# Expert loads on two queues, stores one block later, and a token operand kept in PSUM

## The chip, the cores and the metric

The kernel runs on one core of a Trainium2 chip. The metric is the device time of one execution in microseconds. Three runs of the kernel before gave 5060.06, 5060.66 and 5067.99 us (median 5060.66).

## The reference, cut to what matters

The layer first mixes tokens (attention, a Fourier branch, gates), then mixes channels with PEER, a retrieval over 128 x 128 = 16384 single-neuron experts. The change is in PEER alone:

```
q = hf @ wq                                  # 512 tokens, 8 heads, 2 halves
s = einsum(q, keys);  s1, s2 = top 16 of each half
idx, w = top 16 of the 16 x 16 sums, softmax # 8 x 16 = 128 experts per token
a    = einsum('td,thkd->thk', hf, u[idx])    # up: one dot of length 2048 per pair
coef = w * gelu(a)
out  = einsum('thk,thkd->td', coef, v[idx])  # down
```

All is fp32. `u` and `v` are 16384 x 2048, 134 MB each.

## The kernel before, in words

**Two ways through the experts.** The last 384 tokens (`TD`) are computed densely: for each of the 128 blocks of 128 experts the whole block of `u` is read and multiplied with all 384 tokens, Gelu is applied, and the result goes to a scratch in HBM (`gelu_d`); a second scratch (`route_d`) holds the routing weights, and the down phase multiplies the two. The first 128 tokens (`TS`) are computed sparsely: for each of the 128 slots (head, rank) one row of `u` per token is gathered by an indirect DMA and dotted with that token.

**One dense block i.** `pre_load` (L550) on SyncE issues four DMAs of 256 KB from `peer_u`, one for each quarter of the model dimension; quarter k goes to partitions 32k to 32k+31 of `pu[i % 2]`. VectorE transposes the block in two halves (`u_turn`, L1602, a STREAM_TRANSPOSE of 128 x 1024 into `pT`), ScalarE rounds each half to `pTuh` (`pre_hi`, L1066), GpSimd subtracts to get the low part `pTul` (`u_low`, L718), and TensorE does 48 matmuls of 384 columns (`pre_quarter`, L2232; three products for each of 16 chunks). ScalarE applies Gelu (`pre_gelu`, L1072), and SyncE stores 192 KB (`pre_store`, L557). Every buffer in this line exists twice.

**What sets the order.** Every engine has its order written out by hand, with semaphore waits. Three matter here:

- SyncE (L571 to L632): load of block i+2, store of block i, load of i+3, store of i+1, and so on. The load of i+2 waits until block i has been turned; the store of i waits for Gelu of i (`gelu_set`), and everything behind it on SyncE waits with it.
- ScalarE (`up_block`, L1084): `pre_hi` of block i+1, second half; `pre_hi` of block i+2, first half; then Gelu of block i.
- VectorE: the turn of block i+1's second half may start when the matmuls of block i-1 are done, that of i+2's first half when those of the first half of block i are done.

**Stages of the up phase.** Blocks 0 to 39: VectorE also finds the top experts, four groups of tokens one after the other in stretches of ten blocks (`top_experts`, L1617, with the turns put between its steps); TensorE waits for its end after blocks 19, 29 and 39. Blocks 40 to 63: VectorE also builds one-hot tiles (`one_hots`, L1695), TensorE multiplies them into routing tiles, ScalarE copies these (`keep_route`, L1105), SyncE stores them in pieces of 1 MB (`route_store`, L561); the last four follow after block 63. Blocks 64 to 127 (`LATE` = 64): from block 66 on GpSimd issues gathers of 128 rows of 8 KB (1 MB) into a ring of four buffers (`gather_u`, L727), three per block for four blocks, then two per block; VectorE does one dot for each (`dot`, L1723, a SCALAR_TENSOR_TENSOR of 128 x 2048 with a sum). The ring buffers lie over `route`, so the first gather waits for the last route store. At block 70 SyncE also loads the first operands of the down phase (two `vraw` of 1 MB, two `wt` and two `gel` of 384 KB).

**The token operand.** The matmul operand `h2h`/`h2l` has the model dimension on partitions; chunk c holds, on partition 32w + r, the dimension 512w + 32c + r. The dots need it by token. `tokens_turn` (L2250) turns it on TensorE in blocks 2 to 5: 32 matmuls of 128 columns into the first four PSUM banks, and ScalarE copies them (L1097, in blocks 6 to 9, with the order of the dimension put right) to `h2tok` in SBUF, as [128, 16, 512] of which the first 128 columns of each chunk are used.

Of the kernel before, what the change touches and what calls it, by code (L numbers as in the profile page):

```python
# [119 lines left out]
def layer_kernel(nc, a, out):  # L120
# [10 lines left out]
    with ctx:  # L131
# [119 lines left out]
        h2tok = sb("h2tok", 104, [P, DC, T])  # L251
# [34 lines left out]
        pp = [ctx.enter_context(nc.psum_tensor(f"pp{k}", [P, 1024], fp32)) for k in range(4)]  # L286
# [77 lines left out]

        wmod_v = a["w_mod"][0].rearrange("(c p) n -> p c n", p=P)
# [16 lines left out]
        def _(sp):  # L382
# [161 lines left out]
            u_v = a["peer_u"][0].rearrange("(i j) d -> i j d", j=NK)  # L544
            v_v = a["peer_v"][0].rearrange("(i j) d -> i j d", j=NK)
            u_quarter = [u_v[:, :, QD * k:QD * k + QD].rearrange("i (b s) d -> i s b d", s=32) for k in range(4)]
# [3 lines left out]
            def pre_load(i, s):  # L550
                if not isinstance(i, int) or i >= 2:
                    sp.wait_ge(u_turned, 2 * i - 2)
                for k in range(4):
                    sp.dma_start(pu[s][32 * k:32 * k + 32, :, :],  # L554
                                 u_quarter[k][bass.ds(i, 1)].rearrange("a s b d -> (a s) b d")).then_inc(u_in[s], 16)
# [15 lines left out]
            with sp.Fori(0, P0 // 2) as i:  # L571
                for s in range(2):
                    pre_load(2 * i + 2 + s, s)
                    pre_store(2 * i + s, s)
# [4 lines left out]
            def route_steps(r, first=False):  # L579

                for k in range(8):
                    i = 8 * r + P0 + k
                    pre_load(i + 2, k % 2)
                    if k >= 4:
                        route_store(32 * r + 16, 0, k - 4)
                    elif not first:
                        route_store(32 * r, 1, k)
                    pre_store(i, k % 2)
# [4 lines left out]
            pre_load(LATE + 2, 0)  # L593
            for k in range(4):
                route_store(GROUPS, 1, k)
            pre_store(LATE, 0)
            pre_load(LATE + 3, 1)
            pre_store(LATE + 1, 1)
            with sp.Fori(LATE // 2 + 1, LATE // 2 + 3) as i:
                for s in range(2):  # L600
                    pre_load(2 * i + 2 + s, s)
                    pre_store(2 * i + s, s)
# [26 lines left out]
            with sp.Fori(LATE // 2 + 3, NK // 2 - 1) as i:  # L629
                for s in range(2):  # L630
                    pre_load(2 * i + 2 + s, s)
                    pre_store(2 * i + s, s)  # L632
# [126 lines left out]
        def _(act):  # L759
# [305 lines left out]

            def pre_hi(i, s, h):  # L1066
# [9 lines left out]

            act.wait_ge(mu_red, 64)
            act.activation(identr[:, :], ident[:, :], ACT.Copy)
            pre_hi(0, 0, 0)
            pre_hi(0, 0, 1)  # L1080
            pre_hi(1, 1, 0)
# [28 lines left out]
            def route_part(r):  # L1110

                for k in range(8):
# [3 lines left out]
                    pre_hi(i + 1, 1 - s, 1)  # L1116
# [1267 lines left out]
```

## Time and profile before

| what | us |
|---|---|
| median of three runs | 5060.66 |
| the profiled execution, its own time | 5068.84 |
| its span, first to last instruction | 5067.2 |
| first Gelu of the up phase to the last | 2293.8 to 3860.6 |
| blocks 40 to 63 | about 2750 to 3060 |
| down phase to the end | about 3865 to 5067 |

All times inside the trace are counted from the start of the span. A row of the trace gives the start, the duration, the engine, the line of the kernel and the operation with its output and inputs. SPq, ACTq and so on are an engine's queue, where waits and DMA issues stand. "Releaser" is what ended a wait. A busy share of DMA is the mean over the 16 DMA engines; q1 is the queue of the DMAs that SyncE issues, q0 that of GpSimd's.

### The profile page before, as it was taken

To read this page: it belongs to the slowest core of one execution; us is meant where nothing else is said; L and a number is where in the kernel's file an instruction comes from. 1 tells how busy PE (TensorE), PEld (TensorE's weight loads), DVE (VectorE), ACT (ScalarE), POOL (GpSimd) and SP (SyncE) were. 2 spreads that over 40 slices of the span, in tenths; PEclk is the share of its full clock that TensorE was granted. 3 is DMA by queue.
4 is the path that set the end of the run, shared out by engine and by line. 5 is a ranking of instruction groups with operands and counts; after the bars stand their busy time and mean duration, and the time that the engine had idled before them with its cause. 6 is when DMAs were issued, how large, how long until landed. Compare 5 with 4: busy or idle time off the path is not lost.

```text
span 5067.2 us, 58390 instructions
## 1 busy us (share of the span) xinstructions
PE 4391.1 (87%) x21067; PEld 3686.3 (73%) x21067; DVE 3052.9 (60%) x3412; ACT 1381.0 (27%) x1489; POOL 1591.9 (31%) x643
## 2 busy tenths in 40 slices
PE   7899999999979976898777996677777799999997
PEld 2687777777768865778777996677776677777776
DVE  1234565455436535457667995566665677787777
ACT  0322332333321121322223442122222233332222
POOL 0002331000003300224444435677774233333330
PEclk9899999999999988899999998999999899999998
DMA  8325663000116552664444779899997889989895
GB/s 280 91 83 169 181 185 116 30 29 19 35 55 193 179 125 73 151 142 108 109 107 100 167 175 257 266 281 279 280 282 260 304 335 335 336 329 341 327 343 179
DMA packets 716548, 967.20 MB, mean 191 GB/s; under 512 B 137467, under 2 KB 535859, under 8 KB 680371
## 3 DMA queue, kind: packets, MB, share of 16 engines
q1 hardware_dynamic: 675395, 680.41, 46.3%
q0 software_dynamic: 40928, 285.23, 15.2%
q8 instruction: 45, 0.74, 0.1%
q10 hardware_dynamic: 144, 0.52, 0.0%
q14 instruction: 36, 0.29, 0.0%
HBM read 896.84 MB, written 69.22 MB: 191 GB/s over the span
## 4 chain that ended last, share of the span: by engine, by line
DMA 22%; DVE 13%; issue 7%; SPq 5%; PE 4%; ACT 1%; POOL 0%; DVEq 0%; ACTq 0%; POOLq 0%
DMA gel<-gelu_scratch 11%; DMA pu<-in_peer_u_dram 11%; DVE acc L1749 3%; DVE oneJ L1700 3%; DVE pT L1607 3%; SPq L554 3%; DVE vDl L1418 3%; PE pp L115 1%; PE pp L116 1%; PE pp L117 1%; ACT act_g L1075 1%; SPq L559 1%; SPq L608 0%; SPq L615 0%; DVE oneI L1701 0%
## 5 line engine op out<-in xcount | busy, mean ns | idle before, releaser
L115 PE MATMUL pp<-h2h,pTuh 128*128 128x384 f32 x2048 | 736.3, 360 | 270.3 <-POOL pTul L721 269.4
L721 POOL TENSOR_TENSOR pTul<-pT,pTuh 128x1024 fp32r<-128x1024 f32 x256 | 695.5, 2718 | 603.0 <-ACT pTuh L1070 601.6
L116 PE MATMUL pp<-h2l,pTuh 128*128 128x384 f32 x2048 | 711.0, 347 | 0.0
L117 PE MATMUL pp<-h2h,pTul 128*128 128x384 f32 x2048 | 711.0, 347 | 0.0
L115 PE MATMUL pp<-vDh,coh 128*128 128x512 f32 x1536 | 614.6, 400 | 97.6 <-DVE col L1418 97.2
L115 PEld LDWEIGHTS pp<-h2h,pTuh 128*128 128x128 f32 x2048 | 404.8, 198 | 312.8 <-POOL pTul L721 286.3
L116 PE MATMUL pp<-vDl,coh 128*128 128x512 f32 x1536 | 608.7, 396 | 0.0
L117 PE MATMUL pp<-vDh,col 128*128 128x512 f32 x1536 | 607.3, 395 | 0.0
L1607 DVE STREAM_TRANSPOSE pT<-pu 128x1024 f32<-128x1024 f32 x256 | 317.2, 1240 | 449.2 <-DMA pu<-in_peer_u_dram 385.7
L1070 ACT ACTIVATE pTuh<-pT 128x1024 fp32r<-128x1024 f32 x256 | 271.5, 1060 | 1146.7 <-DVE pT L1607 1146.4
L697 POOL TENSOR_TENSOR mbuf<-mbuf,silu 128x2048 f32<-128x2048 f32 x64 | 261.1, 4080 | 1003.6 <-DMA mbuf<-in_w_mod_dram 1002.9
L735 POOL DMA_INDIRECT ring<-in_peer_v_dram,sidx x128 | 337.2, 2634 | 752.5 <-DVE acc L1749 732.9
L1137 ACT ACTIVATE vDh<-vraw 128x2048 fp32r<-128x2048 f32 x128 | 245.3, 1917 | 670.9 <-PE pp L117 441.0
L1213 DVE TENSOR_TENSOR wl<-wraw,wh 128x2048 fp32r<-128x2048 f32 (+1 forms) x97 | 263.0, 2711 | 270.0 <-ACT wh L797 269.9
L115 PEld LDWEIGHTS pp<-vDh,coh 128*128 128x128 f32 x1536 | 294.9, 192 | 178.8 <-DVE vDl L1418 76.5
L116 PEld LDWEIGHTS pp<-h2l,pTuh 128*128 128x128 f32 x2048 | 405.7, 198 | 0.0
L117 PEld LDWEIGHTS pp<-h2h,pTul 128*128 128x128 f32 x2048 | 403.8, 197 | 0.0
L1725 DVE SCALAR_TENSOR_TENSOR ring<-ring,h2tok 128x2048 f32<-128x2048 f32 x128 | 359.2, 2810 | 0.0
L117 PEld LDWEIGHTS pp<-vDh,col 128*128 128x128 f32 x1536 | 294.9, 192 | 63.3
L116 PEld LDWEIGHTS pp<-vDl,coh 128*128 128x128 f32 x1536 | 295.3, 192 | 60.6
L1418 DVE TENSOR_TENSOR vDl<-vraw,vDh 128x2048 fp32r<-128x2048 f32 x128 | 292.7, 2287 | 64.7 <-ACT vDh L1137 64.6
L115 PE MATMUL pp<-hxh,wh 128*128 128x512 f32 x784 | 316.3, 404 | 13.7 <-DVE wl L1213 9.8
(329 smaller groups left out, 8152.4 us busy)
## 6 DMA issues: line engine op xcount, KB each, us to landing
pu<-in_peer_u_dram SPq DMA_DIRECT2D x512, 256.0 KB, 5.1
vraw<-in_peer_v_dram SPq DMA_DIRECT2D x128, 1024.0 KB, 9.5
mbuf<-in_w_mod_dram SPq DMA_DIRECT2D x64, 1024.0 KB, 5.9
wraw<-in_w_in_dram SPq DMA_DIRECT2D x48, 1024.0 KB, 8.6
wt<-route_scratch SPq DMA_DIRECT2D x128, 384.0 KB, 9.0
gel<-gelu_scratch SPq DMA_DIRECT2D x128, 384.0 KB, 10.4
wm<-in_w_mod_dram SPq DMA_DIRECT2D x16, 2048.0 KB, 8.8
gelu_scratch<-act_g SPq DMA_DIRECT2D x128, 192.0 KB, 1.9
```

What stands on the lines that cost most here:

```text
L115: pe.matmul(out, lh, rh, start=first, stop=False)
L116: pe.matmul(out, lh, rl, start=False, stop=False)
L117: return pe.matmul(out, ll, rh, start=False, stop=last)
L697: pool.tensor_tensor(mbuf[s][:, :, :], mbuf[s][:, :, :], silu[:, :, 0:1].to_broadcast([P, DC, P]), ALU.mult).then_inc(mu_prod, 1)
L721: pool.tensor_tensor(pTul[s][:, c, :], pT[s][:, c, :], pTuh[s][:, c, :].bitcast(fp32), ALU.subtract).then_inc(u_lo, 1)
L735: pool.indirect_dma_start(ring[k % 4][:, :], None, v_rows, bass.IndirectOffsetOnAxis(ap=sidx[:, k:k + 1], axis=0)).then_inc(ring_in[k % 4] ...
L1070: act.activation(pTuh[s][:, 8 * h:8 * h + 8, :], pT[s][:, 8 * h:8 * h + 8, :], ACT.Copy).then_inc(u_hi, 1)
L1137: act.activation(vDh[s][:, :, :], vraw[s][:, :, :], ACT.Copy).then_inc(w_hi, 1)
L1213: dve.tensor_tensor(wl[s][:, 0:n, :], wraw[s][:, 0:n, :], wh[s][:, 0:n, :].bitcast(fp32), ALU.subtract).then_inc(w_lo, 1)
L1418: return dve.tensor_tensor(dst, src, hi.bitcast(fp32), ALU.subtract)
L1607: dve.transpose(pT[s][:, c, :].rearrange("p c (b j) -> p b c j", b=4), pu[s][:, :, 256 * h:256 * h + 256].rearrange("p b (c j) -> p b c j" ...
L1725: dve.scalar_tensor_tensor(out=chunks(ring[k % 4]), in0=chunks(ring[k % 4]), scalar=1.0, in1=h2tok[:, :, 0:TS], op0=ALU.mult, op1=ALU.mult ...
```

## The change

**Loads.** `pre_load` on SyncE issues quarters 0 and 1 only. ScalarE gets a `pre_load` of its own for quarters 2 and 3 (its own DMA queue); it does blocks 0 and 1 before the up phase, block 2 after the first `pre_hi`s, and in `up_block` and `route_part` the load of block i+3 directly behind `pre_hi` of block i+1's second half.

**Stores.** SyncE starts with the loads of blocks 0 to 3 and the store of block 0; from there load i+2 is followed by the store of i-1 instead of i. The route stores are put in three groups instead of four, and the last four come behind the store of block 64 instead of behind the load of block 66.

**Token operand.** `h2tok` is now the first 2048 columns of PSUM (the four banks that `tokens_turn` writes). `tokens_turn` writes it in natural order: each of the 32 matmuls becomes four of 32 columns. The four copies on ScalarE are gone, and the dots read PSUM.

```
@@ layer_kernel
-        h2tok = sb("h2tok", 104, [P, DC, T])
-        pp = [ctx.enter_context(nc.psum_tensor(f"pp{k}", [P, 1024], fp32)) for k in range(4)]
+        ps = ctx.enter_context(nc.psum_tensor("ps", [P, 4096], fp32))
+        pp = [ps[:, 1024 * k:1024 * k + 1024] for k in range(4)]
+        h2tok = ps[:, 0:D]
@@ sync
             def pre_load(i, s):
                 if not isinstance(i, int) or i >= 2:
                     sp.wait_ge(u_turned, 2 * i - 2)
-                for k in range(4):
+                for k in range(2):
...
             pre_load(0, 0)
             pre_load(1, 1)
-            with sp.Fori(0, P0 // 2) as i:
+            pre_load(2, 0)
+            pre_load(3, 1)
+            pre_store(0, 0)
+            with sp.Fori(1, P0 // 2) as i:
                 for s in range(2):
                     pre_load(2 * i + 2 + s, s)
-                    pre_store(2 * i + s, s)
+                    pre_store(2 * i + s - 1, 1 - s)
...
                     pre_load(i + 2, k % 2)
-                    if k >= 4:
-                        route_store(32 * r + 16, 0, k - 4)
-                    elif not first:
-                        route_store(32 * r, 1, k)
-                    pre_store(i, k % 2)
+                    pre_store(i - 1, (k - 1) % 2)
+                    if k >= 5:
+                        for part in ((0, 1), (2,), (3,))[k - 5]:
+                            route_store(32 * r + 16, 0, part)
+                    elif 1 <= k < 4 and not first:
+                        for part in ((0, 1), (2,), (3,))[k - 1]:
+                            route_store(32 * r, 1, part)
...
             pre_load(LATE + 2, 0)
+            pre_store(LATE - 1, 1)
+            pre_load(LATE + 3, 1)
+            pre_store(LATE, 0)
             for k in range(4):
                 route_store(GROUPS, 1, k)
-            pre_store(LATE, 0)
-            pre_load(LATE + 3, 1)
-            pre_store(LATE + 1, 1)
@@ scalar
+            def pre_load(i, s):
+                for k in range(2, 4):
+                    act.dma_start(pu[s][32 * k:32 * k + 32, :, :],
+                                  u_quarter[k][bass.ds(i, 1)].rearrange("a s b d -> (a s) b d")).then_inc(u_in[s], 16)
...
-            def up_block(i, s, exp=None):
+            def up_block(i, s, exp=None, load=True):
                 pre_hi(i + 1, 1 - s, 1)
+                if load:
+                    pre_load(i + 3, 1 - s)
...
-                if 6 <= i < 10:
-                    k = i - 6
-                    act.wait_ge(h2_turned, DC + 4)
-                    act.activation(h2tok[:, :, 0:TS].rearrange("p (a k) (c r) -> p k a c r", a=4, c=4)[:, k],
-                                   pb[k][:, :].rearrange("p (c a r) -> p a c r", c=4, a=4), ACT.Copy).then_inc(h2_hi, 1)
@@ vector
-                dve.scalar_tensor_tensor(out=chunks(ring[k % 4]), in0=chunks(ring[k % 4]), scalar=1.0,
-                                         in1=h2tok[:, :, 0:TS], op0=ALU.mult, op1=ALU.mult,
+                dve.scalar_tensor_tensor(out=ring[k % 4][:, :], in0=ring[k % 4][:, :], scalar=1.0, in1=h2tok, op0=ALU.mult, op1=ALU.mult,
                                          accum_out=dots[:, k:k + 1]).then_inc(ring_used, 1)
@@ tensor
-                    o = pb[k][:, P * (c % 4):P * (c % 4) + P]
-                    pe.matmul(o, h2h[:, c, 0:TS], identr[:, :], start=True, stop=False)
-                    mm = pe.matmul(o, h2l[:, c, 0:TS], identr[:, :], start=False, stop=True)
+                    for w in range(4):
+                        o, e = pb[w][:, 32 * c:32 * c + 32], identr[:, 32 * w:32 * w + 32]
+                        pe.matmul(o, h2h[:, c, 0:TS], e, start=True, stop=False)
+                        mm = pe.matmul(o, h2l[:, c, 0:TS], e, start=False, stop=True)
```

## Rows read from the trace of the kernel before

**Rows 1.** Windows: stretch, length, busy of PE, PEld, DVE, ACT, POOL; clock, DMA share, GB/s.

```profile
2293.80:2745.00 451.20, 356.98 (x1910) 345.24 (x1908) 311.07 (x885) 111.53 (x133) 205.80 (x78) 0.93 0.46 108
2750.00:3060.40 310.40, 307.29 (x1932) 285.67 (x1931) 306.18 (x527) 149.38 (x167) 126.52 (x48) 1.00 0.73 164
3060.40:3208.50 148.10, 92.18 (x461) 89.31 (x460) 72.35 (x52) 23.24 (x29) 86.69 (x39) 0.82 0.91 271
3208.50:3846.10 637.60, 494.92 (x2545) 467.15 (x2544) 413.42 (x319) 132.31 (x160) 497.53 (x212) 0.95 0.94 278
```

**Rows 2.** Timeline of PE in block 3 (matmuls of one block, then of the turn).

```profile
2311.06 0.39 PE L115 MATMUL pp<-h2h,pTuh 128*128 128x384 f32 x1
...
2319.44 0.22 PE L2253 MATMUL pp<-identr,h2h 128*128 128x128 f32 x1
...
2319.61 0.27 PE L2253 MATMUL pp<-identr,h2h 128*128 128x128 f32 x1
2319.72 0.28 PE L2254 MATMUL pp<-identr,h2l 128*128 128x128 f32 x1
```

**Rows 3.** The chain of waits, 2533 to 2560: start, us, what.

```profile
2538.53 6.28 DMA pu<-in_peer_u_dram
2544.93 1.26 DVE pT L1607
...
2547.17 0.48 ACT act_g L1075
2547.81 0.37 SPq L559
...
2548.47 0.32 SPq L554
```

**Rows 4.** The chain of waits, 3400 to 3440.

```profile
3407.66 7.62 DMA pu<-in_peer_u_dram
...
3420.61 6.58 DMA pu<-in_peer_u_dram
```

**Rows 5.** The span.

```profile
core 0 of [0], span 5067.2 us
```

**Rows 6.** Waits in 2273 to 2765: total us, times, longest.

```profile
PE pp L2267 <- DVEq L1691: 42.5, 3, 14.6
```

**Rows 7.** Timeline of SP, then of POOL, at the boundary after block 63.

```profile
3063.59 14.12 SPq L566 DMA_DIRECT2D route_scratch<-route  x4
...
3084.34 1.09 POOL L730 DMA_INDIRECT ring<-in_peer_u_dram,sidx  x1 [19.12 <-DMA route_scratch<-route]
```

**Rows 8.** DMA queues in 4000 to 4800, the down phase.

```profile
q1 hardware_dynamic: 50830, 170.11, 59.2%
q0 software_dynamic: 13687, 99.62, 31.1%
```

**Rows 9.** DMA queues in 3208.5 to 3846.1: packets, MB, share of 16 engines.

```profile
q0 software_dynamic: 15277, 111.25, 50.5%
q1 hardware_dynamic: 38160, 66.01, 43.2%
```

**Rows 10.** DMA queue q1 in 2293.8 to 2745.

```profile
q1 hardware_dynamic: 28080, 48.57, 46.3%
```

**Rows 11.** DMA queue q1 in 900 to 1300, loads over all 128 partitions.

```profile
q1 hardware_dynamic: 6336, 11.01, 8.1%
```

**Rows 12.** Groups by shape: VectorE with one operand in PSUM.

```profile
L1382 DVE TENSOR_TENSOR pTl<-pp,pTh 128x768 fp32r<-128x768 f32 x64 | 61.0, 953 | 49.7 <-ACT pTh L894 48.9
L1334 DVE TENSOR_TENSOR kTl<-pp,kTh 128x512 fp32r<-128x512 f32 x24 | 16.6, 692 | 72.6 <-ACT kTh L868 72.6
```

**Rows 13.** Groups in 3200 to 3800: busy us, mean ns; idle before.

```profile
L721 POOL TENSOR_TENSOR pTul<-pT,pTuh 128x1024 fp32r<-128x1024 f32 x101 | 283.4, 2806 | 118.4 <-ACT pTuh L1070 117.4
...
L1725 DVE SCALAR_TENSOR_TENSOR ring<-ring,h2tok 128x2048 f32<-128x2048 f32 x100 | 276.5, 2765 | 0.0
L730 POOL DMA_INDIRECT ring<-in_peer_u_dram,sidx x100 | 189.3, 1893 | 15.6 <-issue 12.9
```

**Rows 14.** The gathers of u (L730), issue to landing.

```profile
DMA to landing us min/median/max: 5.4/7.9/13.1
```

More of the change, by code:

```diff
@@ L363, in layer_kernel @@
         block = ctx.enter_context(nc.Block())
+        u_v = a["peer_u"][0].rearrange("(i j) d -> i j d", j=NK)
+        u_quarter = [u_v[:, :, QD * k:QD * k + QD].rearrange("i (b s) d -> i s b d", s=32) for k in range(4)]
         wmod_v = a["w_mod"][0].rearrange("(c p) n -> p c n", p=P)
@@ L542, in _ @@
             sp.dma_start(iota[:, :], a["k_iota"]).then_inc(iota_in, 16)
-            u_v = a["peer_u"][0].rearrange("(i j) d -> i j d", j=NK)
             v_v = a["peer_v"][0].rearrange("(i j) d -> i j d", j=NK)
-            u_quarter = [u_v[:, :, QD * k:QD * k + QD].rearrange("i (b s) d -> i s b d", s=32) for k in range(4)]
             for ss in g_stored:
@@ L601, in _ @@
                     pre_load(2 * i + 2 + s, s)
-                    pre_store(2 * i + s, s)
+                    pre_store(2 * i + s - 1, 1 - s)
             def v_load(n, s, half):
@@ L631, in _ @@
                     pre_load(2 * i + 2 + s, s)
-                    pre_store(2 * i + s, s)
+                    pre_store(2 * i + s - 1, 1 - s)
+            pre_store(NK - 3, 1)
             pre_store(NK - 2, 0)
@@ L1075, in pre_gelu @@
                 act.activation(act_g[s][:, :], pb[4 + s][:, 0:TD], ACT.Gelu).then_inc(gelu_set, 1)
+            act.wait_ge(sc_done, 2 * PH)
+            pre_load(0, 0)
+            pre_load(1, 1)
             act.wait_ge(mu_red, 64)
@@ L1080, in _ @@
             pre_hi(0, 0, 1)
+            pre_load(2, 0)
             pre_hi(1, 1, 0)
-            def up_block(i, s, exp=None):
+            def up_block(i, s, exp=None, load=True):
                 pre_hi(i + 1, 1 - s, 1)
+                if load:
+                    pre_load(i + 3, 1 - s)
                 if exp is not None:
@@ L1116, in route_part @@
                     pre_hi(i + 1, 1 - s, 1)
+                    pre_load(i + 3, 1 - s)
                     for q in range(RI):
@@ L1125, in _ @@
                 route_part(r)
-            with act.Fori(LATE // 2, NK // 2 - 1) as i:
+            with act.Fori(LATE // 2, NK // 2 - 2) as i:
                 for s in range(2):
                     up_block(2 * i + s, s)
+            up_block(NK - 4, 0)
+            up_block(NK - 3, 1, load=False)
             pre_hi(NK - 1, 1, 1)
@@ L1717, in _ @@
                     route_block(2 * r + P0 + s, s, 8 * r + 4 * s)
-            def chunks(t):
-                return t[:, :].rearrange("p (c d) -> p c d", c=DC)
             def dot(k):
                 dve.wait_ge(ring_in[k % 4], 16 * (k // 4) + 16)
-                dve.scalar_tensor_tensor(out=chunks(ring[k % 4]), in0=chunks(ring[k % 4]), scalar=1.0,
-                                         in1=h2tok[:, :, 0:TS], op0=ALU.mult, op1=ALU.mult,
+                dve.scalar_tensor_tensor(out=ring[k % 4][:, :], in0=ring[k % 4][:, :], scalar=1.0, in1=h2tok, op0=ALU.mult, op1=ALU.mult,
                                          accum_out=dots[:, k:k + 1]).then_inc(ring_used, 1)
-            dve.wait_ge(h2_hi, DC + 4)
+            dve.wait_ge(h2_turned, DC + 4)
             for i in range(LATE, NK):
```

## The prediction

> **What bounds the kernel now.** Everything that the diff touches lies in the up phase, so I read that phase alone. The windows [rows 1] cut it in four; dividing the matmul counts by 48 per block (less 32 for the token turn in the first) gives 39, 24, 9 to 10 and 53 blocks. So a block takes 451.2/39 = 11.6 us beside the top-expert search, 310.4/24 = 12.9 us beside routing, and 637.6/53 = 12.0 us beside the gathers. Against that TensorE needs 8.38 us for a block at full clock: from 2311.06 to 2319.44 it runs one without a gap [rows 2]. In the first and last stretch it is thus idle or slow for a quarter to a third of the time, and VectorE is no bound either (311 of 451 us, 413 of 638).
>
> The chain of waits says what is. In the first stretch [rows 3] it is a closed loop through a single load: the Gelu (0.48 us) lets the store go (0.37), the load is issued behind it (first of four issues at 2548.47), its data take 6.28 us after the last issue, the turn 1.26, and the next Gelu can only come behind the rounding of that turn, because ScalarE's order puts it there. From Gelu to Gelu in such a loop it is 11 to 12 us. Beside the gathers the same loop stands with 7.62 and 6.58 us of transfer [rows 4]. In the routing stretch VectorE is busy 306 of 310 us [rows 1]: no load ends a wait there that matters. In the last stretch the DMA engines are busy 0.94 of the time [rows 1], so there the loop has a second bound close behind it.
>
> **The change part by part.** The profiled execution (5068.8 us, its span 5067.2 [rows 5]) stands 8.2 us above the median of 5060.66; I sum against the first and subtract 8 at the end.
>
> *Store one block behind the load, stretch 1.* Load i+3 now needs Gelu i-1 and the turn of i+1, which is where load i+2 stood before. It is thus issued one block earlier in relation to its use, and the closed loop spans two blocks: 11.6/2 = 5.8 us per block, no longer a bound. Next late are TensorE at 8.38 us and VectorE at 311/39 = 8.0 us. Two engines so evenly loaded, one of them with steps of uneven length between its turns, don't overlap perfectly. I take 39 x 8.38 = 327, 4 for two waits at ends of the search (now 14 us each [rows 6], because the last turn waits for the same loads; then about 2), 8 for uneven steps, and 8 for the token turn (below): 347 us, a gain of 104. Bounds: 39 x 8.38 + 4 = 331 (gain 120) and 10.0 us per block = 390 (gain 61).
>
> *Two loads on ScalarE.* Two issues of 0.32 us plus gaps, about 1 us per block on an engine busy 112 of 451 us here and 149 of 310 beside routing [rows 1]: hidden by its idle time; if that were gone it would cost 1 us per block. What queues behind them is the next rounding, and behind that GpSimd and TensorE, which then have a block's time in hand.
>
> *Token turn and its copies.* 128 matmuls for 32. The 128-column ones stand 0.11 us apart [rows 2], most of it the change of weights, which stays. Upper bound 96 x 0.11 = 10.6 us, lower 0 if they scale with columns; I take 8, nearer the row. The four copies leave ScalarE's idle time: nothing.
>
> *Routing stretch.* VectorE's work is the same: 0. The route stores move among the loads; half a block of lateness is hidden by a slot being free for four blocks.
>
> *Boundary, 3060 to 3208.* The first gather waits 19.12 us for the last route stores, which SyncE issues from 3063.59 during 14.12 us [rows 7] with two loads behind them. Now they follow the store of block 64, some 8 us later; the loads of 66 and 67 stand ahead of them. The stretch moves 148.1 x 271 GB/s = 40.1 MB. At 335 GB/s, about what the down phase moves ((170.1 + 99.6) MB / 800 us = 337 [rows 8]), that takes 120 us: 28 less, minus 8 = 20 us. Bounds 0 and 35.
>
> *Beside the gathers, 53 blocks.* The loop is gone here too, and the DMA engines become the bound, so their time per MB decides. Now: q1 0.432 x 637.6/66.0 = 4.17 us per MB, q0 0.505 x 637.6/111.3 = 2.89 [rows 9]; per block 1.245 and 2.10 MB, so 5.19 + 6.08 = 11.27 us of work in 12.03. In stretch 1, with nothing beside them, the same loads cost 4.30 us per MB [rows 10], while loads that spread one DMA over all 128 partitions cost 0.081 x 400/11.0 = 2.94 [rows 11]: what is slow is the form, each quarter into 32 partitions, one after another. With quarters 0, 1 on one queue and 2, 3 on the other, two sets of partitions are written at once. If that undoes the loss wholly (2.94, and 2.50 for gathers as in the down phase [rows 8]) the work is 3.66 + 5.25 = 8.9 us, 9.5 at today's share of 0.94; if not at all it is 11.27, 11.5 at a share of 0.98. I take the middle of the two works, 10.1, at 0.98: 10.3 us per block, a gain of 53 x 1.73 = 92. Bounds 28 and 134.
>
> Here row and skill part. The loads' rows above suggest that two halves written at once run faster. The Trainium skill, SBUF — State Buffer, section "Can I just issue two DMAs to hit both halves?", says that one DMA on each half of the partitions gained only 6% over a single one, from whichever engines they are issued. By that rule the DMA work stays, and the result is the first rival's. No row of this case has two such queues.
>
> *Dots from PSUM.* VectorE with one operand in PSUM takes 692 ns for 512 elements and 953 for 768 [rows 12], so 2.26 us for 2048, against 2.77 now [rows 13]: 128 x 0.5 = 65 us less work on an engine with idle time, worth nothing directly. GpSimd now has 2 x 2.81 + 2 x 1.89 = 9.4 us of work per block [rows 13], under 10.3, but nearly all of 9.5. It would shrink if these slow each other today. The Trainium skill, SBUF — State Buffer, "Who interferes with whom", says that a VectorE instruction with two SBUF inputs contends with GpSimd's reads and one with a single SBUF input does not; by that, GpSimd has room also at 9.5, the second rival.
>
> **Sum.** 5068.8 - 104 - 20 - 92 = 4853; less 8: **4845 us**.
>
> **The rivals.**
> - *A second queue buys time, not rate.* DMA work stays at 11.27 us per block. For it: the DMA share is 0.94 already. Against it: 4.30 against 2.94 us per MB. Gains 104 + 12 + 28 = 144: 4917.
> - *The rate comes back wholly.* 9.5 us per block, 26 at the boundary: 5068.8 - 104 - 26 - 134 - 8 = 4797. Against it: rows at 2.94 and 2.50 are from stretches with less mixing of sizes.
> - *VectorE's order is the next wait in stretch 1.* The search's steps between two turns reach several us; 10.0 us per block gains 61 instead of 104: 4888.
> - *The gathers starve, slower than before.* u now has two queues of three, and a dot that waits for its gather holds the turns behind it on VectorE. Four ring buffers serve two blocks, so a block can't be shorter than half of landing + dot (2.3) + wait behind GpSimd's subtractions (up to 6). To eat the 124 us of the rest, 53 blocks must take 14.4 us, so the landing must exceed 20 us; it is 7.9, at most 13.1 [rows 14]. At 22 us: 15.2 us per block, 5060.7 - 124 + 53 x 3.1 = 5101.
> - *It doesn't do what it says.* If ScalarE's half of each load is issued behind a wait as late as before, the loop stays: 5061. Its place ahead of the rounding of i+2 speaks against that.
>
> **How the numbers follow.** Chances: forecast 0.40; no rate gained 0.27; rate whole 0.12; VectorE's order 0.13; starved 0.03; not as it says 0.03; 0.02 for others, of either sign. Range: the first rival's 4917 with 23 more for a stretch 1 short of its sum gives 4940, and the second's 4797 with a few us for the lower bounds gives 4790; what lies outside is the last two and the tails. A measurement of this kernel can tell 0.2% (10 us) from no change: faster 0.94, same 0.02, slower 0.04.
>
> **What the profile after would show.** Stretch 1: the wait of TensorE at L2267 falls from 14 us to about 2, a block takes near 9 us, and PE or DVE lead the chain instead of DMA pu. Routing stretch: still 12.9 us per block; if it changed, my "0" there is wrong. Boundary: the route stores' issue some 8 us later after the Gelu of block 63. Beside the gathers: q1 and the new queue together well under 4.17 us per MB, a DMA share near 0.98, GB/s near 325, the dot near 2.26 us. A share of 0.98 at 4.17 us per MB is the first rival; idle time of VectorE before L1725 with landings above 20 us the fourth. A block of 12 us in stretch 1 makes the whole reading wrong.

## The result, and the profile after

The changed kernel takes **4793.03 us** (median of four runs, 4787.55 to 4800.62) against 5060.6: ratio 0.9469, 95% interval 0.9452 to 0.9486, 5.3% less. The forecast was 4845 in a range of 4790 to 4940. The profiled execution is one of the four and took 4789.41 us. The windows of the changed kernel, in the columns of [rows 1] and cut at the same Gelus (block 0 to 39, 40 to 63, 63 to 72, 72 to 125):

```profile
2290.10:2642.90 352.80, 347.82 (x2006) 346.50 (x2004) 313.39 (x885) 112.03 (x130) 209.04 (x79) 0.98 0.53 137
2659.90:2956.70 296.80, 290.99 (x1856) 273.53 (x1855) 295.41 (x502) 146.86 (x163) 122.67 (x47) 1.00 0.68 167
2956.70:3078.70 122.00, 80.61 (x424) 79.66 (x423) 59.94 (x52) 23.86 (x29) 62.44 (x39) 0.80 0.98 313
3078.70:3570.10 491.40, 459.16 (x2563) 449.38 (x2562) 358.41 (x319) 132.56 (x159) 356.27 (x213) 0.99 1.03 361
```

Cut at the same Gelus, the kernel before has 451.3, 297.8, 148.2 and 637.6 us. The phase after the last Gelu is nearly as long as it was (1206.6 before, 1204.0 after), so nothing was given back later. By stage the change saves 98.5, 1, 26 and 146 us; 3.7 more lie before the first Gelu, 1.5 in the pieces between the stretches and behind block 125.

- **First stretch:** TensorE is busy 347.8 of 352.8 us (357 of 451 before), so TensorE is now its bound. A block takes 9.05 us with the token turn in it.
- **Routing stretch:** VectorE is busy 295.4 of 296.8 us, as before. The stretch didn't move.
- **Beside the gathers:** A block takes 9.27 us instead of 12.03, at 361 GB/s instead of 278, and the DMA share is 1.03. TensorE is busy 459 of the 491 us, so it stands close behind.

Two views name what holds a block in the last stretch. First its DMA queues (packets, MB, share of 16 engines; q1 is SyncE's, q10 ScalarE's), which answer to [rows 9]:

```profile
q0 software_dynamic: 15325, 111.66, 61.5%
q1 hardware_dynamic: 22868, 38.16, 24.3%
q10 hardware_dynamic: 15187, 27.64, 17.3%
```

Loads of u and stores of Gelu together: (0.243 + 0.173) x 491.4/65.8 = 3.11 us per MB, 4.17 before. Gathers: 0.615 x 491.4/111.7 = 2.71, 2.89 before. (Such a figure is worked out from the share and the length of the window, so the parts always add up to the block's time again. It says where engine time went, and it can be compared between kernels; it is not a price that belongs to a transfer.) Then the chain of waits, 3300 to 3340 (start, us, what), which answers to [rows 4]:

```profile
3306.13 13.07 DMA pu<-in_peer_u_dram
3319.23 1.25 DVE pT L1623
...
3329.07 2.26 DVE ring L1738 x2
3331.34 1.17 DVE pT L1623
...
3333.21 13.61 DMA pu<-in_peer_u_dram
```

From one load to the next on this chain it is 27.08 us, in which three blocks are done. The Gelu and the store are gone from it. In their place stand GpSimd's subtraction, the matmuls of a half block and a dot. A load takes twice as long as in [rows 4], 13 us against 7, and yet the block is shorter and the rate higher, which fits more transfers being under way at once. Last the groups of this stretch, which answer to [rows 13]:

```profile
L728 POOL TENSOR_TENSOR pTul<-pT,pTuh 128x1024 fp32r<-128x1024 f32 x106 | 254.4, 2400 | 118.4 <-ACT pTuh L1082 116.6 <-issue 0.7
L1738 DVE SCALAR_TENSOR_TENSOR ring<-ring,ps 128x2048 f32<-128x2048 f32 x107 | 240.7, 2249 | 0.0
...
L737 POOL DMA_INDIRECT ring<-in_peer_u_dram,sidx x107 | 102.6, 959 | 16.6 <-issue 11.4
```

The dot fell from 2765 to 2249 ns, as computed. Unforeseen in size: GpSimd's subtraction fell from 2806 to 2400 ns, and its issue of a gather from 1893 to 959 ns.

### The profile page after: what moved, and what is told of

Its sections match the earlier page's. It is cut to its first block, busy times and chain, and to the rows that moved or that the text cites. A ratio compares the mean times of both kernels' runs of the same rounds, so it can differ in the third digit from the quotient of the medians.

```text
span 4787.7 us, 58551 instructions
## 1 busy us (share of the span) xinstructions
PE 4331.5 (90%) x21163; PEld 3663.4 (77%) x21163; DVE 2986.1 (62%) x3412; ACT 1384.7 (29%) x1485; POOL 1407.8 (29%) x643
## 4 chain that ended last, share of the span: by engine, by line
PE 45%; DMA 21%; DVE 19%; issue 7%; ACT 4%; SPq 2%; POOL 1%; DVEq 1%; ACTq 0%; POOLq 0%
PE ps L115 14%; PE ps L116 13%; PE ps L117 13%; DMA gel<-gelu_scratch 11%; DMA pu<-in_peer_u_dram 7%; DVE acc L1761 3%; DVE oneJ L1716 3%; DVE vDl L1434 3%; DVE pT L1623 2%; DMA wm<-in_w_mod_dram 2%; PE ps L1881 1%; DVE mred L1314 1%; DVE ring L1738 1%; PE ps L2039 1%; ACT wh L804 1%
## 5 line engine op out<-in xcount | busy, mean ns | idle before, releaser
L115 PE MATMUL ps<-h2h,pTuh 128*128 128x384 f32 x2048 | 708.4, 346 | 87.0 <-POOL pTul L728 86.0
L115 PE MATMUL ps<-vDh,coh 128*128 128x512 f32 x1536 | 615.1, 400 | 93.9 <-DVE col L1434 93.3
L117 PE MATMUL ps<-h2h,pTul 128*128 128x384 f32 x2048 | 695.5, 340 | 0.0
L116 PE MATMUL ps<-h2l,pTuh 128*128 128x384 f32 x2048 | 695.3, 339 | 0.0
L116 PE MATMUL ps<-vDl,coh 128*128 128x512 f32 x1536 | 609.6, 397 | 0.0
L117 PE MATMUL ps<-vDh,col 128*128 128x512 f32 x1536 | 608.1, 396 | 0.0
L115 PEld LDWEIGHTS ps<-h2h,pTuh 128*128 128x128 f32 x2048 | 393.0, 192 | 98.4 <-POOL pTul L728 84.4
L116 PEld LDWEIGHTS ps<-h2l,pTuh 128*128 128x128 f32 x2048 | 393.2, 192 | 0.0
L117 PEld LDWEIGHTS ps<-h2h,pTul 128*128 128x128 f32 x2048 | 392.2, 192 | 0.0
L115 PE MATMUL ps<-hxh,wh 128*128 128x512 f32 x784 | 314.9, 402 | 13.8 <-DVE wl L1229 9.9
```

The lines of the kernel that those rows point to most:

```text
L115: pe.matmul(out, lh, rh, start=first, stop=False)
L116: pe.matmul(out, lh, rl, start=False, stop=False)
L117: return pe.matmul(out, ll, rh, start=False, stop=last)
```

## The experiments

Theory one: the new order opened the closed loop; the two halves of the partitions raised the rate of the loads; the PSUM operand gave time to engines that had some anyway. Theory two: a second queue gives time but no rate, so that something else made the last stretch short. The change has three parts with two forms each: order, queues, operand. That gives eight kernels, two of which were there; six runs complete them, and six more follow up single points.

### One queue

```
-                for k in range(2):      # SyncE; ScalarE's own pre_load is left out
+                for k in range(4):
```

> The changed kernel with all four quarters of each load issued by SyncE, in SyncE's new order (store one block behind); ScalarE issues none. Theory H (halves): the rate beside the gathers came from writing both halves of the partitions at once, so one queue falls back to about 4.2 us per MB, 11.0 to 11.5 us per block in the 53 blocks beside the gathers (changed kernel: 491.4/53 = 9.27), and the total is 4793 + 53 x 1.9 = about 4890; the first 39 blocks stay near 353 us. Theory F (in flight): the rate came from a second load being under way early, whatever the queue, so the total stays at 4793 within 15 us.

4857.15 us (4847.48 to 4863.57), ratio 0.9597 (0.958 to 0.9613). First stretch 351.7 us, as with two queues. Beside the gathers 10.47 us per block. Its queues there, over 554.8 us:

```profile
q0 software_dynamic: 15389, 112.05, 61.4%
q1 hardware_dynamic: 38099, 65.88, 41.8%
```

3.52 us per MB. The second queue is thus worth nothing in the first stretch, and 63 us in the last, where the DMA share is 1.03 with either. The total fell between the two theories (4890 and 4793).

### Two queues, other pairs

```
-                for k in range(2):      # SyncE
+                for k in (0, 2):
-                for k in range(2, 4):   # ScalarE
+                for k in (1, 3):
```

> The changed kernel with the quarters paired otherwise: SyncE issues 0 and 2, ScalarE 1 and 3, so that each queue writes to both halves of the partitions one after the other, and the two queues are on the same half whenever they run in step. Theory H with lockstep: most of the gain in rate is lost, 10.3 to 11.3 us per block, total 4850 to 4895. Theory Q (two queues are enough, because their transfers drift apart): 9.3 to 9.5 us per block, total within 15 us of 4793.

4832.78 us (4825.02 to 4836.23), ratio 0.955 (0.9534 to 0.9566). 10.32 us per block over 547.1 us:

```profile
q0 software_dynamic: 15402, 112.16, 61.0%
q1 hardware_dynamic: 22943, 38.27, 24.7%
q10 hardware_dynamic: 15241, 27.75, 17.7%
```

0.424 x 547.1/66.0 = 3.51 us per MB: the value of one queue. Two queues whose quarters alternate gain 8 us of those 63. The other 55 come with the pairs: queue one loads quarters 0 and 1, queue two 2 and 3. Two things are tied together in that. The pairs split the partitions that are written into a lower and an upper half, and since quarter k also reads its own quarter of each row of `u`, they split the rows that are read as well. No run takes these apart; where the text says "halves", it means both.

The loads are less than half of it. From this run to the changed kernel a block's loads fall by 1.245 x 0.40 = 0.50 us of engine time, and its gathers, 2.98 us per MB here and 2.71 there, by 2.10 x 0.27 = 0.57.

### The old order

```
# SyncE's sequence as before: load i+2, store i; route stores as before
# quarters 2 and 3 stay on ScalarE, issued as in the changed kernel
```

> The changed kernel with SyncE's order of before (store of block i directly behind the load of block i+2; route stores as before); ScalarE still issues quarters 2 and 3 early. Theory order (the closed loop through one load is what bound the first stretch): SyncE's two quarters are late as before, but only half of the bytes hang on them, so the loop is shorter by 2 to 3 us: 8.9 to 9.6 us per block, 350 to 375 us for 39 blocks, beside the gathers 9.5 to 10.2, total 4810 to 4860. Theory rate (what bound was the transfer rate alone): no loss, 4793 within 10 us. If the loop is not shortened at all by the other queue: 430 us for 39 blocks and about 12 us beside the gathers, total near 5010.

4933.81 us (4925.39 to 4964.62), ratio 0.9772 (0.9738 to 0.9807). First stretch 406.9 us, boundary 149.0, 10.52 us per block beside the gathers. Half of each load is still issued behind the store of its block, and that half closes the loop. The early half shortens it only from 11.6 to 10.4 us, less than I expected: the total lies outside the ranges of all three theories, between the first and the third.

### The operand of the dots in SBUF

```
-        h2tok = ps[:, 0:D]
+        h2tok = sb("h2tok", 104, [P, DC, T])   # turn of 128 columns, four copies, dots as before
```

> The changed kernel with the token operand of before: 32 matmuls of 128 columns, four copies on ScalarE, dots with both operands in SBUF. Both theories: the first 39 blocks gain 12 to 18 us (no 32-column matmuls, no clock drops behind them). Theory P (the PSUM operand takes VectorE and GpSimd apart): the dot goes back to 2.77 us, GpSimd's work to 9.4 us per block and its issue gaps make it the bound, 9.7 to 10.0 us per block, +23 to +39, total 4800 to 4820. Theory not needed (DMA is the bound, GpSimd has room): 9.3 us per block, total 4775 to 4783.

4870.44 us (4865.6 to 4873.88), ratio 0.9625 (0.9609 to 0.9641). First stretch 337.4 us, 15.4 less; beside the gathers 10.80 us per block. The window of that stretch, and two of its groups:

```profile
3071.60:3643.90 572.30, 472.15 (x2545) 438.41 (x2544) 572.30 (x319) 132.50 (x160) 554.24 (x213) 1.00 0.93 308
```

```profile
L1746 DVE SCALAR_TENSOR_TENSOR ring<-ring,h2tok 128x2048 f32<-128x2048 f32 x107 | 460.4, 4303 | 0.0
L737 POOL DMA_INDIRECT ring<-in_peer_u_dram,sidx x106 | 299.7, 2828 | 16.9 <-issue 16.9
```

VectorE is busy for all 572.3 us and GpSimd for 554. The same dot took 2765 ns in the kernel before; now that both engines have work all the time it takes 4303, and each gather's issue 2828. By themselves neither would fill a block of 10.8 us: at the durations of [rows 13] GpSimd has 9.4 us and VectorE 2 x 2.77 + 2 x 1.24 = 8.0. So the operand's place, which I had priced at nothing, is worth 77 us; the total lies well above the ranges of both theories.

How they slow each other is to be seen in single rows. First the kernel before, then this run (start, us, engine, line, operation):

```profile
3403.14 2.25 DVE L1725 SCALAR_TENSOR_TENSOR ring<-ring,h2tok 128x2048 f32<-128x2048 f32 x1
3406.48 3.27 DVE L1725 SCALAR_TENSOR_TENSOR ring<-ring,h2tok 128x2048 f32<-128x2048 f32 x1
3404.39 3.21 POOL L721 TENSOR_TENSOR pTul<-pT,pTuh 128x1024 fp32r<-128x1024 f32 x1 [2.21 <-ACT pTuh L1070]
3407.75 2.83 POOL L730 DMA_INDIRECT ring<-in_peer_u_dram,sidx  x1 [0.15 <-issue]
3413.16 0.95 POOL L730 DMA_INDIRECT ring<-in_peer_u_dram,sidx  x1 [0.16 <-issue]
```

```profile
3405.26 4.30 DVE L1746 SCALAR_TENSOR_TENSOR ring<-ring,h2tok 128x2048 f32<-128x2048 f32 x1
3405.01 2.40 POOL L728 TENSOR_TENSOR pTul<-pT,pTuh 128x1024 fp32r<-128x1024 f32 x1
3407.57 2.83 POOL L737 DMA_INDIRECT ring<-in_peer_u_dram,sidx  x1 [0.16 <-issue]
```

In the kernel before a dot takes 2.25 us when it starts on its own, which is what a dot with its operand in PSUM takes; the mean of 2765 is a mixture of these and of 3.27. In the run here the dot starts at 3405.26, GpSimd's subtraction ends at 3407.41, and the dot ends 2.15 us behind that. The gather is issued at 3407.57 and ends 0.84 us behind the dot, where an undisturbed issue takes 0.95. In the kernel before, too, the dot of 3.27 us ends 2.15 behind the subtraction of 3.21 (3407.60 to 3409.75). So in these rows the two engines take turns, instruction by instruction. Every half block repeats it, 5.40 us (3405.01 to 3410.41), and two of them are the 10.80 us of the block. That the dot takes 2.25 us from SBUF in the same form also rules out the other difference between the two dots, that the SBUF operand is read in pieces of 128.

### The order alone, and the queues alone

```
# order alone: one queue (as above) and the operand in SBUF (as above)
# queues alone: the old order (as above) and the operand in SBUF
```

> The change in SyncE's order alone: all four quarters on SyncE, store one block behind, token operand as before in SBUF. Expected by the runs so far: first 39 blocks 335 to 340 us (as with the operand in SBUF and two queues), beside the gathers VectorE and GpSimd hold each other up: 10.8 us per block or a little over, like with two queues, since the DMA engines (3.5 us per MB, 10.5 us per block) are no longer the tightest bound; total about 4865 to 4885. If instead the two bounds add up: 11.5 us per block, total 4910.

4868.47 us (4860.07 to 4876.45), ratio 0.9635 (0.9612 to 0.9657): 337.2 us in the first stretch, 10.88 per block in the last, where VectorE is busy 545 of 577 us and its dot takes 4034 ns. The DMA share is 1.02 there, against 0.93 with two queues, so here both bounds are near.

> The kernel before with the two queues alone: order of SyncE as before (load i+2, store i), operand of the dots in SBUF. It completes the eight combinations. From the runs with the old order and the PSUM operand: stretch 1 took 406.9 us there with 32-column turns that cost some 15, so 392 here (451 before). Beside the gathers the dot goes back to over 3.5 us under load, and the new order with this operand took 10.8 to 10.9 us per block with VectorE full; here the loop through the load adds to it: 11.2 us per block, range 10.9 to 11.6. Total: 5058 - 59 - 53 x 0.8 = some 4955 us. If halves alone were worth nothing without the PSUM operand, it would be 12.0 us per block and 4999.

4967.89 us (4945.75 to 4982.05), ratio 0.9832 (0.9797 to 0.9867): 395.0 us, then 11.53 per block. It came out slower than I expected by 13 us. Beside the gathers its loads cost 4.15 us per MB, no less than before. Halves don't raise the rate in every kernel; more on that below.

### The PSUM operand alone

```
# the kernel before, with h2tok = ps[:, 0:D], the turn of 32 columns and the dots from PSUM
```

> The kernel before with the token operand in PSUM alone (128 matmuls of 32 columns, no copies, dots from PSUM); loads and stores as before. Theory loop: with every load behind the Gelu of the block before, the loop through one load hides VectorE's and GpSimd's work, so beside the gathers it stays at 11.9 to 12.1 us per block and the total at 5060 within 20 us. Theory port: the two engines' holding each other up cost time already before, so the 53 blocks fall to 10.8 us, total about 5000.

5123.02 us (5113.26 to 5137.62), ratio **1.0137** (1.011 to 1.0165): a part that takes work away from two engines, and the kernel is slower by 66 us, which neither theory had. Nearly all of the loss lies behind block 63: the boundary took 163.5 us (148.2), and a block beside the gathers 13.0 (12.03); the first stretch is 3.4 us longer. Its window there, then its chain of waits from 3400 to 3440, then GpSimd's timeline in the same place:

```profile
3228.60:3917.40 688.80, 518.09 (x2540) 502.15 (x2541) 359.14 (x319) 132.23 (x160) 353.29 (x212) 0.88 0.85 257
```

```profile
3407.47 8.10 DMA pu<-in_peer_u_dram
...
3420.89 9.54 DMA pu<-in_peer_u_dram
...
3435.50 7.88 DMA pu<-in_peer_u_dram
```

```profile
3407.04 0.96 POOL L731 DMA_INDIRECT ring<-in_peer_u_dram,sidx  x1 [0.15 <-issue]
3408.01 2.42 POOL L722 TENSOR_TENSOR pTul<-pT,pTuh 128x1024 fp32r<-128x1024 f32 x1
3410.59 0.96 POOL L731 DMA_INDIRECT ring<-in_peer_u_dram,sidx  x1 [0.16 <-issue]
```

Every engine is idle longer, and the transfers on the chain are longer than those of [rows 4]. Over the whole stretch VectorE waits 329.7 us for loads, 224.2 before. In the kernel before the same two gathers stand at 3407.75 for 2.83 us and at 3413.16 (rows above): there the dot slowed GpSimd, and the second gather left behind the load's last issue by over 5 us. Here both are issued within 3.6 us, right behind the load on which the loop waits. That suggests a collision; the next run tests it.

### The same, with the gathers issued later

```
-                gather_u(first of the block)
                 u_low(i, i % 2, 0)
-                gather_u(the others)
                 u_low(i, i % 2, 1)
+                gather_u(all of the block)
```

> The kernel before with the PSUM operand alone (which took 5123 us, 13.0 us per block beside the gathers against 12.03 before), now with both gathers of a block issued by GpSimd behind both of its subtractions instead of one ahead of them and one between. Theory, collision: the quicker GpSimd issued its gathers right behind the one load on which the closed loop waits, and shared the DMA engines with it (transfers of 7.9 to 9.5 us on the chain against 6.6 to 7.6). Gathers that start later leave the load more of the engines: transfers on the chain back near 7 us, 12.2 us per block or less, some 5075 us. Rival, the start of the gathers is not it: 12.8 to 13.1 us per block, 5115 to 5125. Rival two, gathers now come too late and VectorE waits for them: over 13.3 us per block, over 5140, with idle time of VectorE before the dots.

5044.68 us (5035.38 to 5058.6), ratio 0.999 (0.9976 to 1.0004): 70 us less than the run above, each taken against the kernel before in its own round, and 11.60 us per block. The chain of waits, 3400 to 3440:

```profile
3410.92 6.02 DMA pu<-in_peer_u_dram
...
3422.79 5.81 DMA pu<-in_peer_u_dram
...
3434.57 5.76 DMA pu<-in_peer_u_dram
```

The loads take 5.8 to 6.0 us instead of 7.9 to 9.5, with the same transfers and the same engines' work, and VectorE waits 255.8 us for them instead of 329.7. One could think that the subtractions, which come earlier now, shorten the loop. They don't: GpSimd and TensorE are on the chain in neither run, and what lies between two transfers on it got longer, 5.9 us for 5.1 to 5.3. So the collision is shown. (It gained more than the 12.2 us per block that I expected.)

### Two ways to turn the tokens cheaper

The first puts the 32-column turn, eight matmuls at a time, behind the quarters of a block. The second turns 128 columns at a time, copies them on ScalarE to SBUF in blocks 6 to 9, and from there to PSUM in natural order ahead of the dots.

```
# first:  after each quarter of blocks 2 to 5: token_turn(chunk)
# second: act.activation(h2tok[:, 512 * k:512 * k + 512], h2sb[:, 4 * k:4 * k + 4, 0:TS], ACT.Copy)
```

> The changed kernel with the token turn cut up: the 8 small matmuls of one chunk behind each quarter of blocks 2 to 5, instead of 32 behind each block. Theory clock: the three drops of the granted clock that stand behind the turns (3.4 us at half speed each) come from 3.5 us of 32-column matmuls in one piece; spread, they go, 5 us less in the first 39 blocks (348), total 4788. Theory no effect: 353 and 4793.

> The changed kernel with the token turn of before (32 matmuls of 128 columns, four copies to SBUF on ScalarE) and four more copies on ScalarE from SBUF to the PSUM banks, after which the dots read PSUM. Expected: the first 39 blocks at 337 us as with the operand in SBUF, beside the gathers 9.3 us per block as in the changed kernel, total 4793 - 15 = 4778. If ScalarE's copies delay a block: up to 5 us more.

4783.18 us (4779.34 to 4801.33), ratio 0.9466 (0.9443 to 0.9489), and 4774.56 us (4765.82 to 4780.47), ratio 0.9438 (0.9418 to 0.9458). The first stretch took 347.3 and 337.4 us, against 352.8. Both came out as expected. The cause is to be seen in the changed kernel. Each of the first three windows below is a turn and the block behind it, from block 2's turn on; the next two windows lie directly behind the turn of the second; the last rows are TensorE's timeline in such a turn:

```profile
2306.70:2318.60 11.90, 11.90 (x82) 11.90 (x81) 7.61 (x37) 2.61 (x3) 4.76 (x3) 1.00 0.45 107
2318.60:2332.10 13.50, 13.50 (x83) 13.50 (x82) 10.99 (x28) 2.62 (x4) 4.77 (x3) 0.87 0.36 93
2332.10:2345.60 13.50, 13.50 (x82) 13.50 (x82) 8.42 (x27) 2.65 (x4) 4.80 (x3) 0.87 0.39 92
2322.10:2323.50 1.40, 1.40 (x6) 1.40 (x6) 1.40 (x3) 0.50 (x1) 0.00 (x0) 0.60 0.00 0
2323.50:2325.00 1.50, 1.50 (x6) 1.50 (x6) 1.50 (x6) 0.56 (x1) 0.87 (x1) 0.50 0.40 76
```

```profile
2318.57 0.26 PE L2266 MATMUL ps<-identr,h2h 128*128 128x32 f32 x1
2318.68 0.26 PE L2267 MATMUL ps<-identr,h2l 128*128 128x32 f32 x1
```

The small matmuls stand 0.11 us apart like those of [rows 2], so 96 more cost 10.6 us. In addition the granted clock falls behind three of the four runs of 32 of them, from 1.00 (2.4 GHz) to 0.50 (1.2 GHz). The mean over such a window is 0.87, that is (1 - 0.87)/0.5 x 13.5 = 3.5 us at the lower level, though TensorE was never idle, and the window is 1.6 us longer for it. Behind the first run the clock stays at 1.00; why, no run shows. With the turn spread among the quarters it stays at 1.00 throughout, and 5.5 us come back. The second way is the fastest kernel of the study; its lead over the changed kernel is shown by the first stretch, while the intervals of the totals overlap.

### The early loads of the down phase in two parts

In the changed kernel two stops stand at the boundary: from the Gelu of block 65 to the next it is 29.2 us, and from block 69's 33.5. In the kernel before the same two are 17.6 and 31.1 us, so the first has grown while the blocks around it got shorter. SyncE's timeline has the second:

```profile
3027.75 7.79 SPq L555 DMA_DIRECT2D pu<-in_peer_u_dram  x2
...
3039.96 8.86 SPq L555 DMA_DIRECT2D pu<-in_peer_u_dram  x2
```

Beside the gathers two issues take 0.82 to 0.88 us; here they take 8 to 9, directly behind the early loads. On top of the best kernel, half of these loads were moved to block 76:

```
             v_load(0, 0, 0)
-            v_load(1, 1, 0)
             coef_loads(0, 0, 0)
-            coef_loads(1, 1, 0)
# both come six blocks later instead
```

> The turn of 128 columns with copies to PSUM (4774.6 us), and in addition the down phase's early loads of block 70 in two parts: vraw 0 with its wt and gel at block 70, vraw 1 with its own at block 76. In the changed kernel SyncE's issues of two loads of u took 7.79 and 8.86 us there and Gelu 70 to 71 took 33.6 us where a block takes 9.3. Theory, a bubble: the queue of SyncE is full for 24 us and nothing else of the chain can go on, so two smaller bumps hide in the slack of one block: a gap of under 15 us, total 4755 to 4762. Rival, bytes: these loads are work of a DMA resource that is full anyway (its share is 1.03), so the total is the same wherever they stand: 4770 to 4780, with the gap shorter but the blocks behind it longer.

4780.15 us (4776.52 to 4796.85), ratio 0.9476 (0.9454 to 0.9499). The stop behind block 69 is 28.3 us (34.3 in the best kernel), and a new one of 24.7 stands behind block 75. Blocks 63 to 125 took 627.4 us together, against 619.4. Nothing was gained, and the total is the one that the second theory gave. SyncE's issues of two loads now take 0.82 to 1.22 us around both places, and the stops are there all the same, so the full queue accounts for 6 us of the stop at most. That the stretch pays for the bytes wherever they stand fits all of this.

### Late gathers in the best kernel

```
# the edit of the gathers above, on the turn of 128 columns with copies to PSUM
```

> The turn of 128 columns with copies to PSUM (4774.6 us, 9.37 us per block beside the gathers, clock there 0.98), and in addition both gathers of a block issued behind both subtractions of GpSimd, which had taken the kernel with the old order from 13.0 to 11.6 us per block by shortening the one load on its chain. Theory, bytes: with two queues and the new order the DMA resource is full whatever the order of the issues (share 1.03, VectorE waits 2.6 us per block for loads, but never for gathers), so it stays at 9.3 to 9.5 us per block, 4768 to 4782 us. Rival one, the order of the issues matters here too: loads that are met by fewer gathers arrive earlier and TensorE's 8.4 us come nearer: 9.0 us per block or less, 4755 or less. Rival two, gathers issued later leave the DMA engines idle in places and the dots wait: over 9.8 us per block, over 4797.

4823.3 us (4811.65 to 4860.79), ratio 0.9559 (0.9526 to 0.9592), 10.10 us per block. What shortened the old order by 70 us makes the new one longer by 48. That is the second rival, over 9.8 us per block and over 4797 us. The longest waits in its last stretch that a transfer ended (engine and line, what for, total us, times, longest):

```profile
DVE ring L1746 <- DMA ring<-in_peer_u_dram,sidx: 168.3, 91, 2.7
```

In the best kernel VectorE waits there 137.9 us for loads of u and hardly for gathers; here its waits are all for gathers. The rate fell from 358 to 330 GB/s, and the loads, in halves as before, cost 3.50 us per MB instead of 3.14.

### The eight kernels side by side

| order | queues | operand | ratio | first stretch, us | last, us per block |
|---|---|---|---|---|---|
| old | one | SBUF | 1 | 451.3 | 12.03 |
| old | one | PSUM | 1.0137 | 454.7 | 13.00 |
| old | two | SBUF | 0.9832 | 395.0 | 11.53 |
| old | two | PSUM | 0.9772 | 406.9 | 10.52 |
| new | one | SBUF | 0.9635 | 337.2 | 10.88 |
| new | one | PSUM | 0.9597 | 351.7 | 10.47 |
| new | two | SBUF | 0.9625 | 337.4 | 10.80 |
| new | two | PSUM | 0.9469 | 352.8 | 9.27 |

Alone the three parts change the time by -3.65%, -1.68% and +1.37%: -3.96% in sum. Together it is -5.31%. With the operand in SBUF the second queue gives the new order nothing (0.9635, 0.9625; the intervals overlap): the DMA share falls from 1.02 to 0.93, but VectorE and GpSimd, by turns, take 10.8 us per block. With the operand in PSUM the second queue gives 1.3%.

## Why the prediction was right, and where it was wrong

*What bounds the kernel: right.* The closed loop through Gelu, store and load was the bound of the first stretch. The order alone brings that from 451.3 to 337.2 us, with one queue. The wait of TensorE at the ends of the search within this stretch went from 29.1 us in two (the 42.5 of [rows 6] count a third, at its end) to 4.9 in two, longest 2.4, as forecast.

*First stretch: right in sum, one term mis-sized.* Forecast gain 104 us, measured 98.5. The kernels without the 32-column turn give the rest: 337.2, 1.8 us under my term without it (347 - 8 = 339). The term "token turn, 8 us, bounds 0 to 10.6" was wrong beyond its bound: it costs 15.4 (352.8 against 337.4). 10.6 is the spacing, which is all that I counted. The other 5 is the clock (three windows, each 1.6 us longer), which I didn't think of as part of the price.

*Routing stretch, 0: right.* 297.8 and 296.8 us.

*Boundary: right, 26 us for 20, for a part of the reason.* The first gather waited 24.80 us for the route stores, 19.12 before: later by 5.7 us, for 8 forecast. The rate rose to 313 GB/s, below the 335 that I took from [rows 8]; fewer bytes lay in the stretch (122.0 x 313 = 38.2 MB for 40.1).

*Beside the gathers: the term that was mis-sized.* It reads "I take the middle of the two works, 10.1, at 0.98: 10.3 us per block". The work is 1.245 x 3.11 + 2.10 x 2.71 = 9.56 us at a share of 1.03: 9.27, and the gain 146 us for 92. Its 54 us are the miss of the total (52); the other terms' errors nearly cancel. It came out below the 9.5 of the second rival, beyond my bound of 134. Half of the miss per block is work (9.56 for 10.1 us), half the share. Two things were wrong in it. The share of 0.98 was a guess at what can be reached; by this counter it is 1.03, and it stands at 1.02 or 1.03 in all kernels with the new order and the PSUM operand but one (the late gathers, 1.00). A value above 1 also says that it is no strict measure of how full the engines are. And the middle was taken between "no gain" and "wholly back" with nothing that spoke for the middle; the argument of the halves, by which 3.66 of 8.9 us was u, was nearly right (3.87).

*The total: in the range, in part by luck.* It lies 3 us above the range's lower end and 4 from the second rival's 4797, whose chance I put at 0.12. That rival's terms are not what was measured either: 8.9 us of work at a share of 0.94, against 9.56 at 1.03. And 77 of the 268 us that the kernel gained hang on the PSUM operand, which the sum has at nothing.

*The first rival (a second queue buys time, not rate, 4917): fell in the last stretch.* The trace of before could not tell it from the forecast. By the rule of the Trainium skill, SBUF — State Buffer, section "Can I just issue two DMAs to hit both halves?", one DMA on each half gains 6% over one. In the first stretch this case comes near that: in the new order 3.86 us per MB with halves, 4.31 with alternating quarters and 4.23 with one queue, 9% less than with one, on engines that are half idle. Beside the gathers it does not: 3.11 with halves, 3.51 with the same two queues and alternating quarters, 3.52 with one. Here the measurement decides: halves are worth 11% of the loads' engine time, 9% of the gathers', and 1.05 us per block (against alternating quarters). With the old order, though, two halves cost 4.15 us per MB beside the gathers against 4.17 with one queue (operand in SBUF), and 3.98 against 4.27 (in PSUM). In the new order the SBUF operand alone raises one queue's figure from 3.52 to 4.08, and late gathers raise that of the halves from 3.14 to 3.50. So what a load costs in engine time depends on what is under way beside it, and halves pay most in the new order. Why that is so no run here separates.

*Dots from PSUM, "worth nothing directly": wrong.* The duration was right (2.26 forecast, 2.25 measured), though for another reason than I thought: it is also what an undisturbed dot takes from SBUF, and the 2.77 was a mean over disturbed ones. The room of VectorE and GpSimd was not right: I computed it from durations at the old pace. The interference that the Trainium skill names (same page, "Who interferes with whom": an instruction of VectorE with two SBUF inputs contends with GpSimd's reads) is what the runs show, with 2765 ns at 12.0 us per block and 4303 at 10.8. It was in the text as an aside about the second rival; it should have been a rival of its own for the kernel without the PSUM operand, and a term for the one with it.

*The starved gathers: not seen in the changed kernel,* where VectorE waits for loads. The late gathers in the best kernel show that this edge is near: put both issues of a block behind the subtractions, and all of VectorE's waits are for gathers.

## What to carry to other kernels

A loop of load, compute and store through one queue is opened by storing one step behind; that alone gave two thirds of the gain (3.65 of 5.31%), and the closed loop is to be seen in the chain of waits before anything is changed. A price for "less work on an engine with idle time" holds at the pace of the trace; when other parts shorten the step, contention between two engines can make both the bound (here 9.4 and 8.0 us of work became 10.8). Look at single rows and not at the mean: where one instruction comes in two durations, 2.25 and 3.27 us, ask what it waits for, and add up what takes turns. And when the step is not shortened, a quicker engine may issue its transfers into the one transfer that all wait for (here 66 us slower). Where parts of a change act on the same transfers, test them in pairs, and read the transfers' time on the chain as well as their sum.

## What the runs showed of the hardware

- A VectorE dot of 128 x 2048 with both inputs in SBUF took 2.25 us undisturbed, and on the mean 2.77, 3.31, 4.03 and 4.30 us as the block went from 12.0 to 11.5, 10.9 and 10.8 us; with one in PSUM it took 2.25 (2.28 with late gathers) at 9.3 to 13.0 us per block. GpSimd's issue of an indirect DMA, no arithmetic, is hit as much: 0.96 us beside the second, up to 2.83 beside the first. In the rows of the run with the SBUF operand the dot ended 2.15 us behind the end of GpSimd's subtraction, and the issue 0.84 us behind the end of the dot.
- Behind three of four runs of 32 matmuls of 32 columns TensorE's granted clock fell to 0.50 (mean 0.87 over 13.5 us) with TensorE busy throughout. In the kernel with eight at a time among larger ones it stayed at 1.00.
- 32-column matmuls stood 0.11 us apart, no closer than 128-column ones.
- A load's time to land says little of the rate: 7 us at 278 GB/s, 13 us at 361.
- Issuing can take long where much is under way: four route stores took 15.55 us of SyncE's time in the changed kernel and two loads of u behind them 3.92; behind the down phase's early loads two loads of u took 7.79 and 8.86 us.
